# Opening of a fused attention, mixer and expert kernel: identity first, token tiles one by one, lambda in the loop

## The reference, cut to what matters

```
shift, scale, gate = split(silu(c) @ w_mod + b_mod, 3)
shift_c, scale_c   = split(silu(c_ctx) @ w_mod[:, :2*D] + b_mod[:2*D], 2)
hx = x   * rsqrt(mean(x*x)     + 1e-6) * norm_g * (1 + scale)   + shift
hc = ctx * rsqrt(mean(ctx*ctx) + 1e-6) * norm_g * (1 + scale_c) + shift_c
lam = exp(sum(lam_q1*lam_k1)) - exp(sum(lam_q2*lam_k2)) + 0.2
keys, and all later projections: hx @ w_in, hc @ w_in[:, ...]
```

## Time and profile before

| | |
|---|---|
| median of 3 runs | 2855.74 us (2848.79 to 2856.3) |
| the profiled execution, its own time | 2853.2 us |
| its span, from the first to the last instruction | 2851.5 us |
| TensorE busy | 2755.9 us, 97% of the span |
| VectorE, ScalarE, GpSimd busy | 60%, 47%, 21% |
| granted TensorE clock, mean | 0.991 |
| first to last square of a token tile (starts) | 14.67 to 20.94 us |
| first transpose, first matmul of mod(0) | 26.12, 36.43 us |

### The profile page before, as it was taken

The page is one execution under the profiler, slowest core; times in us unless marked ns, Lnnn a source line. Parts: engine busy times, 40 slices in busy tenths (PEclk is TensorE's granted clock), DMA queues, the critical chain, the costliest instruction groups (busy, mean ns, idle before and its releaser), DMA issues.

```text
span 2851.5 us, 49868 instructions
## 1 busy us (share of the span) xinstructions
PE 2755.9 (97%) x15744; PEld 2365.3 (83%) x15744; DVE 1710.4 (60%) x3265; ACT 1348.0 (47%) x2555; POOL 601.5 (21%) x504
## 2 busy tenths in 40 slices
PE   5999989999989999999999999999999999999997
PEld 4798768887779889989999888888888888888886
DVE  3456573234674567768888655555556766666666
ACT  3242463225554454545444455455545555555553
POOL 0001010000000000000004877877611111111110
PEclk9999999999999999999999999999999999999998
DMA  8857615373455555565556777778767666666674
GB/s 315 345 170 236 206 48 160 110 317 111 169 178 184 158 179 165 169 184 187 168 183 176 174 184 190 185 184 188 191 212 252 213 219 214 221 213 218 217 244 141
DMA packets 185380, 554.46 MB, mean 194 GB/s; under 512 B 54064, under 2 KB 54112, under 8 KB 181200
## 3 DMA queue, kind: packets, MB, share of 16 engines
q1 hardware_dynamic: 133632, 485.57, 53.3%
q0 software_dynamic: 51664, 67.79, 9.2%
HBM read 532.17 MB, written 21.10 MB: 194 GB/s over the span
## 4 chain that ended last, share of the span: by engine, by line
PE 52%; DVE 1%; ACT 0%; DMA 0%; issue 0%; ACTq 0%; DVEq 0%; SPq 0%
PE PS L2210 12%; PE PS L163 11%; PE PS L164 11%; PE PS L165 11%; PE PS L2212 6%; DMA raw<-in_v 0%; DVE w_lo L154 0%; PE PS L2181 0%; DVE hb L2549 0%; DVE stats L2524 0%; DVE hb L2521 0%; DVE hb L2547 0%; PE PS L257 0%; ACT w_hi L147 0%; ACT L2302 0%
## 5 line engine op out<-in xcount | busy, mean ns | idle before, releaser
L154 DVE TENSOR_TENSOR w_lo<-raw,w_hi 128x512 fp32r<-128x512 f32 x1666 | 1155.1, 715 | 771.5 <-ACT w_hi L147 765.0
L147 ACT ACTIVATE w_hi<-raw 128x512 fp32r<-128x512 f32 x1666 | 1011.0, 629 | 832.3 <-PE PS L165 769.3
L2210 PE MATMUL PS<-h,w_hi 128*128 128x512 f32 x1504 | 533.1, 400 | 2.0 <-DVE w_lo L154 2.0
L2123 POOL DMA_INDIRECT g_dram<-gt,spot x256 | 415.7, 1624 | 345.5 <-DVE gt L2472 237.3
L2212 PE MATMUL PS<-h,w_lo 128*128 128x256 f32 x1504 | 423.1, 281 | 0.0
L163 PE MATMUL PS<-w_hi,wj_hi 128*128 128x512 f32 x1024 | 399.3, 390 | 4.1 <-DVE wj_lo L2269 4.1
L165 PE MATMUL PS<-w_hi,wj_lo 128*128 128x512 f32 x1024 | 398.9, 390 | 0.0
L164 PE MATMUL PS<-w_lo,wj_hi 128*128 128x512 f32 x1024 | 398.9, 390 | 0.0
L2210 PEld LDWEIGHTS PS<-h,w_hi 128*128 128x128 f32 x1504 | 283.4, 188 | 73.1 <-DVE w_lo L154 2.4
L2212 PEld LDWEIGHTS PS<-h,w_lo 128*128 128x128 f32 x1504 | 284.8, 189 | 0.0
L163 PE MATMUL PS<-h,w_hi 128*128 128x256 f32 x800 | 228.3, 285 | 6.5 <-DVE w_lo L154 2.9
(11 more groups left out here) (359 smaller groups left out, 4140.1 us busy)
## 6 DMA issues: line engine op xcount, KB each, us to landing
raw<-in_u_s SPq DMA_DIRECT2D x256, 512.0 KB, 4.4
raw<-in_v SPq DMA_DIRECT2D x256, 512.0 KB, 5.0
raw<-in_w_in_s SPq DMA_DIRECT2D x112, 512.0 KB, 3.9
raw<-in_w_in_b SPq DMA_DIRECT2D x64, 512.0 KB, 4.0
raw<-in_w_out_s SPq DMA_DIRECT2D x64, 512.0 KB, 3.6
raw<-in_w_in_a SPq DMA_DIRECT2D x52, 512.0 KB, 4.3
raw<-in_w_mod_s SPq DMA_DIRECT2D x32, 512.0 KB, 7.0
raw_more<-in_w_mod_s SPq DMA_DIRECT2D x32, 512.0 KB, 7.4
```

The source lines that it names most:

```text
L147: act.activation(w_hi[m % 2][:, half], raw[:, m % NRAW, half], ACT.Copy).then_inc(hi_ready, 1)
L154: dve.tensor_tensor(w_lo[m % 2][:, half], raw[:, m % NRAW, half], w_hi[m % 2][:, half].bitcast(F), ALU.subtract).then_inc(lo_ready, 1)
L2123: pool.indirect_dma_start(g_dram, bass.IndirectOffsetOnAxis(spot[:, t, h, k:k + 1], 0), gt[:, t, h, k:k + 1], None, compute_op=ALU.add).th ...
L2210: pe.matmul(PS[:, 6 + j % 2, :], w_hi[m % 2][:, c], h_both[:, kk, :, :].rearrange("p a t -> p (a t)"), start=(kk == 0), stop=False)
```

## The change

The identity's tile `cst` goes to SP's queue, ahead of `xs`, with a semaphore of its own (`ident_in`), for which the transposes and `pick2` now wait. GpSimd's queue keeps three loads, `bm` first. The lambda arithmetic moves into the loop: VectorE sums after feature tile 2, ScalarE's exponential comes at k = 3, VectorE's difference after feature tile 6; VectorE waits for the three small loads behind its first split of the keys. ScalarE gets an early table load for the root, and it squares a token tile, takes its root, and copies out even groups of the tile before; VectorE takes mean square, norm and copies tile by tile. The squares' scratch tile `junk0` moves from the last quarter of `xT` to the room of `x_lo`, which is first written in the loop.

```
+    sp.dma_start(cst[:, :], io["consts"][:, 0:C_KEEP]).then_inc(ident_in, 16)      # behind cin, ahead of xs
...
-    small_load(pool, cst[:, :], io["consts"][:, 0:C_KEEP])
+    small_load(pool, bm[:, :], io["mod_cols"])
...
     @blk.tensor
-    pe.wait_ge(small, 64)
+    pe.wait_ge(ident_in, 16)
...
     @blk.scalar
-    act.wait_ge(lam_asked, 1)
-    act.activation(lam[:, 2:4], lam[:, 0:2], ACT.Exp).then_inc(lam_given, 1)
+    act.preload_act_table(ACT.Sqrt)
     for t in range(4):
         act.wait_ge(x_in[t], 16)
         if t:
             act.wait_ge(sq, t)
         act.activation(junk[:, :], xs[:, t, :], ACT.Square, accum_out=ms[:, t, 0:1]).then_inc(sq, 1)
-    for t in range(4):
         act.wait_ge(rms_asked, t + 1)
         act.activation(ms[:, t, 2:3], ms[:, t, 1:2], ACT.Sqrt).then_inc(rms_given, 1)
-    for g in range(0, 16, 2):        # copy out group g
+        if t:
+            turn_out(4 * t - 4)
+            turn_out(4 * t - 2)
+    turn_out(12)
+    turn_out(14)
...
+    if k == 3:                       # in the loop, behind rounded(4)
+        act.wait_ge(lam_asked, 1)
+        act.activation(lam[:, 2:4], lam[:, 0:2], ACT.Exp).then_inc(lam_given, 1)
...
     @blk.vector
-    dve.wait_ge(small, 64)           # and the lambda arithmetic
+    dve.wait_ge(ident_in, 16)
     dve.tensor_reduce(pick2, ident ...).then_inc(picks_made, 1)
-    normalise(0)
     for t in range(4):
-        if t < 3:
-            normalise(t + 1)
-        turn_out(4 * t + 1)
-        turn_out(4 * t + 3)
+        mean_square(t)
+        normalise(t)
+        if t:
+            turn_out(4 * t - 3)
+            turn_out(4 * t - 1)
+    turn_out(13)
+    turn_out(15)
...
     key_split(0)
+    dve.wait_ge(small, 48)
     for k in range(KT):
         modulate(k)
         x_rest(k)
+        if k == 2:
+            lambda_asked()
+        if k == 6:
+            lambda_made()
```

More of the change, by code:

```diff
@@ L423, in opening @@
                 roped = nc.alloc_sbuf_tensor_at("roped", [P, 2, 2, T], F, offset=spare + (2 + KB) * T * 4)
-                junk = nc.alloc_sbuf_tensor_at("junk0", [P, D], F, offset=at + 4 * D * 4 + 3 * D * 4)
+                junk = nc.alloc_sbuf_tensor_at("junk0", [P, D], F, offset=x_at + KT * 2 * T * 4)
                 wk_raw = nc.alloc_sbuf_tensor_at("wk_raw", [P, 3, KB * P], F, offset=H_OFFSET)
@@ L437, in opening @@
                 x_in = [sem(f"x_in{i}") for i in range(4)]
-                c_in = sem("c_in")
+                c_in, ident_in = sem("c_in"), sem("ident_in")
                 exp_c, silu_c, sq, rms_asked, rms_given, normed, tr, tr_out, tr_outv, lam_asked, lam_given, picks_made = (
@@ L510, in _ @@
                         clear_last_stage(pool)
-                        small_load(pool, cst[:, :], io["consts"][:, 0:C_KEEP])
+                        small_load(pool, bm[:, :], io["mod_cols"])
                         small_load(pool, lamv[:, :, :].rearrange("p a b -> p (a b)"), bcast(io["lam_in"]))
                         small_load(pool, csta[:, :], io["consts"][:, C_KEEP:C_ALL])
-                        small_load(pool, bm[:, :], io["mod_cols"])
                         pool.wait_ge(key_lo, 2 * KT)
@@ L637, in _, with turn_out @@
                         act.activation(cex[:, :, :], cin[:, :, :], ACT.Exp, scale=-1.0).then_inc(exp_c, 1)
-                        act.wait_ge(lam_asked, 1)
-                        act.activation(lam[:, 2:4], lam[:, 0:2], ACT.Exp).then_inc(lam_given, 1)
                         act.sem_inc(hi_ready, 2 * N_MOD)
+                        act.preload_act_table(ACT.Sqrt)
+                        def turn_out(g):
+                            t, q4 = g // 4, g % 4
+                            act.wait_ge(tr, g + 1)
+                            act.activation(xT[:, 4 * q4:4 * q4 + 4, t * P:(t + 1) * P],
+                                           PS[:, g % 6, :].rearrange("p (k c) -> p k c", k=4), ACT.Copy).then_inc(tr_out, 1)
                         for t in range(4):
@@ L645, in _ @@
                             act.activation(junk[:, :], xs[:, t, :], ACT.Square, accum_out=ms[:, t, 0:1]).then_inc(sq, 1)
-                        for t in range(4):
                             act.wait_ge(rms_asked, t + 1)
                             act.activation(ms[:, t, 2:3], ms[:, t, 1:2], ACT.Sqrt).then_inc(rms_given, 1)
-                        for g in range(0, 16, 2):
[L650 to L653, removed]
+                            if t:
[3 more added lines that the diff above has]
+                        turn_out(14)
                         def key_round(k):
@@ L725, in _, with mean_square @@
                         dve.tensor_copy(c_wide[:, :, :, :], csilu[:, :, :, None].broadcast_to([P, KT, 2, 16])).then_inc(silu_c, 1)
-                        dve.wait_ge(small, 64)
-                        step(dve.tensor_tensor(lamp[:, :, :], lamv[:, 0:4:2, :], lamv[:, 1:4:2, :], ALU.mult))
-                        dve.tensor_reduce(lam[:, 0:2], lamp[:, :, :], X, ALU.add).then_inc(lam_asked, 1)
+                        dve.wait_ge(ident_in, 16)
                         dve.tensor_reduce(pick2[:, :], ident[:, 0:P:16].rearrange("p (j w) -> p w j", w=2), X, ALU.add).then_inc(picks_made, 1)
[L730 to L733, removed]
+                        def mean_square(t):
                             dve.wait_ge(sq, t + 1)
@@ L778, in x_rest, with lambda_asked, lambda_made @@
                             dve.tensor_tensor(x_lo[:, k, :], xT[:, k, :], x_hi[:, k, :].bitcast(F), ALU.subtract).then_inc(x_split, 1)
+                        def lambda_asked():
+                            step(dve.tensor_tensor(lamp[:, :, :], lamv[:, 0:4:2, :], lamv[:, 1:4:2, :], ALU.mult))
+                            dve.tensor_reduce(lam[:, 0:2], lamp[:, :, :], X, ALU.add).then_inc(lam_asked, 1)
+                        def lambda_made():
+                            dve.wait_ge(lam_given, 1)
+                            step(dve.tensor_tensor(lam[:, 4:5], lam[:, 3:4], lam[:, 2:3], ALU.subtract))
+                            dve.tensor_scalar(lam[:, 7:8], lam[:, 4:5], -LAMBDA_INIT, None, ALU.add)
                         key_split(0)
+                        dve.wait_ge(small, 48)
                         for k in range(KT):
```

## The result

The changed kernel takes 2835.06 us (median of 18 runs, 2828.53 to 2848.32), the kernel before in the same sessions 2850.43 us (18 runs, 2840.2 to 2863.22). The ratio is 0.9949, with a 95% interval of 0.9936 to 0.9962: 10.8 to 18.2 us gained. The direction was right and the size too small.

What follows compares the result with a forecast made beforehand. TensorE was taken to bound the kernel, with its 36.43 us prefix paid in full. mod(0) at 25.7 us gains 10.7 us, so 2853.2 - 10.7 = 2842.5, say 2843 us; range 2837 to 2850.

Steps and rivals of the forecast that it cites:

- What bounds the kernel: Whole kernel: TensorE bounds it, so a microsecond counts if it moves the point from which TensorE works without a pause.
- mod(0) at 25.7 us: Opening: mod(0) starts at 25.7 us instead of 36.43, a gain of 10.7 us.
- The last transposes at the high clock: Opening, last token tile: transposes run at the high clock, done at 25.6 us rather than 27.0 at the low one.
- The rival with mod(0) at 27.0 us: Opening: short bursts start cold, last tile turned at 1.2 GHz, gain 9.4 us instead of 10.7; no chance of its own.
- Data just in time: mod(1)'s last slab and the key tile land before they are wanted, with about one us to spare.
- Table load 1.28 us: Opening, ScalarE: the early load for the root falls in idle time, so 1.28 us leave the prefix.
- no reload for each tile: Opening, ScalarE: squares and roots share a table set; the rival of reloads per tile gains 5.1 us, 2848, chance 0.04.
- Lambda in the loop at no cost: Loop: lambda's work fits waits of 2.57 and 2.40 us, cost zero; without that cover 1.5 + 1.1 us once.
- The order behind mod(0) and its distances stay as they were, low clock included: After mod(0): later work keeps its spacing, including TensorE's stretch at clock 0.50, so the gain carries through unchanged.
- The sum from 2853.2 us: Whole time: 2853.2 - 10.7 = 2842.5, say 2843 us, starting from the profiled execution; 2845 from the median.
- The last sign of being wrong: Whole kernel: the forecast is wrong if the shift at 60 us is not found again at the end.
- The rival of a slower kernel: Opening into loop: thinner bursts keep TensorE's clock low; two half-clock passes give 2856 us, three 2862; chance 0.04.

Runs made afterwards that it cites:

- small_loads_late: Changed kernel, but GpSimd issues its three small loads only after the last token tile has landed; ratio to the kernel before 0.9956.
- no_early_table: Changed kernel without ScalarE's early table load for the root; ratio to the kernel before 0.9953, mod(0) at 26.75 us.
- each half: Kernel before with only the identity's queue and lambda's place changed (ratio 0.9982), or only the tile order and early table load (0.9973).
- fillers: Idle identity transposes in mod(2)'s waits: on the changed kernel 0.9957, 0.9920, 0.9947; on before 0.9988; on changed with small loads held back 0.9932.

## Why the prediction was wrong, point by point

- **What bounds the kernel: right.** TensorE's first unbroken work moved, and the end moved with it.
- **mod(0) at 25.7 us: right within 0.9.** Measured 24.8 to 25.3, a gain of 11.5 instead of 10.7 us. The chain came out nearly as worked: squares at 8.74, 12.32, 16.15 and 19.43 against 6.8, 12.2, 15.8 and 19.5, the last tile turned at 23.43 against 23.6, at the high clock. The first tile was 1.9 us late, as the identity's load was put at 0.64 us and cost 1.8 to 2.3. By the prediction the second tile's landing bound the chain; in fact it was the first tile, so that the lateness cost about 0.4 us at mod(0), and too long an estimate elsewhere covered it.
- **The last transposes at the high clock: right.** The sixteen of the last tile took 1.97 us. The rival with mod(0) at 27.0 us didn't come, and by the prediction's own times its condition wasn't given: tiles 1 and 2 were bursts of 3.4 us with pauses of 0.2 to 0.3 us behind them. In the trace after, the last two tiles are bursts of 1.97 us with pauses of 1.6 and 1.3 us ahead, and the clock stayed high.
- **Data just in time: right.** mod(1) didn't wait; mod(2) waited for its slabs as before, and small_loads_late shows how little was to spare.
- **Table load 1.28 us: right within 0.2** (1.1 by no_early_table), and no reload for each tile. **Lambda in the loop at no cost: right.** The exponential sits in the loop's idle time; the timeline of ScalarE after:

```profile
57.75 1.28 ACT L690 ACT_TABLE_LOAD   x1
59.05 0.20 ACT L690 ACTIVATE lam<-lam 128x2 f32<-128x2 f32 x1
60.30 0.94 ACT L666 ACTIVATE w_hi<-wk_raw 128x384 fp32r<-128x384 f32 x2 [1.05 <-DMA wk_raw<-in_w_key_s]
```

  The drain of 1.38 us that the Trainium skill, ScalarE: Activation LUTs, section "What ACT_TABLE_LOAD costs", counts on top of the load isn't there: 0.02 us lie between the instruction ahead, which ends at 57.73 us, and the load, and 0.02 us between the load and the exponential.
- **"The order behind mod(0) and its distances stay as they were, low clock included": this failed.** It held in three of four profiles of the changed kernel and not in the pair's. In the profiled pair it hid 2.6 us, over four profiles of each 1.2 us. I took one execution's low stretch for part of the program.
- **The sum from 2853.2 us, and "about 3 us either way belong to the measurement": this failed too, and with the low stretch it put the time outside the range.** Those 2853.2 us are one execution, and one with the long u loop, as its profile shows. The 3 us I read from three runs of before, 7.5 us apart. Eighteen runs lie 23 us apart, since the u loop alone has two speeds 9.7 us apart and the low stretches vary. The median of before was 2850.43 us and not the 2853.2 us of the profiled execution: 2.8 of the 7.9 us between forecast and result. The other 5.2 us are the gain: 15.4 measured against 10.2 from 2853.2 to the 2843 put down. Of these 0.5 are that rounding, 0.8 mod(0) and 1.2 the low stretch; the rest, 15.4 - 12.7 = 2.7 us, is within the measurement's own interval (10.8 to 18.2 us) and stays unexplained. A larger share of short u loops in the changed kernel's runs could hold it; that was not shown.
- **The last sign of being wrong came true in the profiled pair:** the shift of 13.7 us at 60 us was not found again at the end, where it is 24.7. The u loop's two speeds are 9.7 us of that, and no waiting.

The rival of a slower kernel didn't come: the low stretches were 0, 10.2, 6.8 and 10.2 us long in the changed kernel and 6.8, 6.8, 10.2 and 10.2 us before, and none reached past keys(0).

## What to carry to other kernels

Find the point from which the bounding engine works without a pause, and count the gain there: it was carried nearly unchanged through 1400 us of work. Two edits that clear the same stretch needn't add up: here each half gave 4 us and both 11.5, as each kept alive a wait that the other had to remove. Where a chain starts with several tiles, compare the distance from each tile to the end over several runs: the one that stays constant is the tile that binds. Before a range is drawn, see how far the runs of the unchanged kernel lie apart, and don't count a low stretch of the clock from one profile as part of the program.

## What the runs showed of the hardware

- The same matmul loop, with no wait in it, ran at two speeds: 399 and 393 ns a record, 1134 and 1155 matmuls in 400 us, at a granted clock of 1.00. What chooses the speed is not known.
- The granted clock fell to 0.50 in or after mod(2)'s waits in seven of eight executions of the two kernels, in 12 of 13 without fillers, and in one of five with them.
- Transposes alone brought the clock up: their records shortened from 421 to 272 ns at 30.6 us before and at 17.0 us after, when TensorE had done nothing but transposes, since 26.12 and 12.82 us. The clock column of the windows shows 1.00 ahead of that too, so there the level is read from the records' length.
- One load of 256 KB on SP's queue ahead of the tiles moved the first square from 6.4 to between 8.2 and 9.1 us, more than the 0.64 us that its bytes take at 407 GB/s, while the second stayed at 12.0 to 12.4 us in all but no_early_table, where the table load stood ahead of it.
